# Hybrid decoder layer on one core: sample output product in three column parts, prompt probabilities scaled by GpSimd before plain transposes, value products two turns behind

## Chip, cores and metric

The kernel runs on one core of one Trainium2 chip. The metric is the device time of one execution in microseconds (us). The measurement tells a change of about 0.5% from none. Engines are named PE (TensorE; PEld is its weight load), DVE (VectorE), ACT (ScalarE), POOL (GpSimd) and SP (SyncE, which issues all DMAs here).

## What is computed

One decoder layer over a prompt (2048 positions) and 64 sample rows (8 sequences of 8 new positions, each with a cache of 2048). Model width 1024; the mixer has 6 attention heads of width 64 (A), an RG-LRU (B) and 6 HGRN2 heads (C). The change touches part A only, and of it two things: the prompt's attention after the softmax, and the product of probabilities and cached values for the samples.

```
h = rmsnorm(x); z = h @ w_in                     # q, k, v, gates of A, B and C
A, prompt: three strided branches per head, (window, dilation) = (128,1), (512,4), (2048,16)
    p_b = exp(q k^T / 8 - max_b);  o_b = p_b v / sum(p_b)
    o   = sum_b weight_b * o_b,  weight_b ~ denominator of branch b    (softmax over log-sum-exps)
    mixed_A = o * silu(gate)
A, sample: the same for 8 new rows of each of 8 sequences against cache + new keys
y = x + concat(mixed_A, mixed_B, mixed_C) @ w_out;  y = rmsnorm(y)
```

## The kernel before

The program has two parts. `front` (0 to about 1110 us of the profile) makes the input projections and parts B and C of the prompt; the change does not touch it. `attend_project` does the rest. Its order of work is a hand-written list of steps, made by `attend_schedule` and `project_schedule`; every engine walks the same list and issues its own share of each step, in order, and the engines meet at semaphores.

**Prompt attention.** The 2048 positions are held in 4 residue classes (position modulo 4), so that a row block `i` (0 to 3) is 512 positions. A head has 32 units `u` = (h, i, far, m): a unit is one 128-row score tile, near (128 or 256 keys) or far (128 times i+1 keys). For a unit PE makes two products (keys split into a high and a low part, L2446 and L2447) into one of three banks `sp_`, DVE adds the mask and takes the extreme (L2223), and ACT takes the exponential in place in the probability tiles `pna`, `pnb` and `pf` (L2071). After a head's last unit the steps `w`, `x` and `z` compute the merge weights of near and far, one number per query row and branch, in `wt` (L2160, L2284; semaphore `weights`).

Then come the head's 18 turns. A turn takes a group of up to four 128x128 probability blocks. Step `t` is one matmul for each block, with the block as stationary operand and a diagonal matrix as moving operand: this transposes the block and scales each query row by its weight at once (L2515, into bank `tp[n % 2]`). POOL makes the diagonals from the identity, eight per row block (L1978, tile `diag`). ACT copies three turns of four to `pt` in SBUF, DVE the fourth (L1601, L1603, in `evacuate`). Step `o` multiplies values and transposed block (L2538) into an accumulator `op` of 64 rows, those of the head's parity. In the list, `o` of turn n-1 follows `t` of turn n. When the four row blocks of a head are done, one after the other, each has a step `f`: DVE multiplies by the gate (L2294, 64x512) and SP stores it to the array `mab` (L1852). The turns of head h begin 11 units into head h+1 (`LEAD`), so they are laced with that head's units; those of the last head have no units beside them, only the nine steps `pw` that split `w_out` (ACT L2082, DVE L2300). The q and k of the next head are read and split in the steps `s` (ACT L2029, DVE L2208 and L2212).

**Projection and samples.** `project_schedule` laces 34 half-tiles `pp` of the output product (27 matmuls of 128x512 each, helper lines L49 to L51) with the attention of eight samples. For sample b: `sr` POOL multiplies 2304 columns of far keys by the query (L1992), `sk` scores, `sm` transposes the probabilities into `ptt`, `so` the output product (L2581): for each of 11 key tiles one matmul of all 48 probability columns (6 heads x 8 rows) with all 384 value columns, of which only a head's own 64 are used. DVE copies 48x384 to `orow` (L2360), `sb` turns it back in three transposes (L2587). `pt` and `split_mixed` prepare a tile of the mixed activations: its A part is read from `mab` once the stores of step `f` have landed (`load_mixed`).

## Time and profile before

| | |
|---|---|
| median of 3 runs | 1864.3 us (1863.65 to 1872.5) |
| profiled execution | 1865.9 us, of which span 1864.2 us |
| mean granted PE clock | 0.98 of 2.4 GHz |
| PE, DVE, ACT, POOL busy | 93%, 54%, 48%, 35% |
| prompt attention with turns | about 1222 to 1510 us |
| projection and samples | about 1510 to 1864 us |

Busy shares are averages over stages with different limits, so they say little about one stage. A record "MATMUL ... 0.27 us" is the latency of one pipelined matmul; what a matmul costs a stream is the distance from its start to the next one's start. A float32 product of two full operands shows as two records, a transpose through the identity as one.

### The profile page before, as it was taken

Reading aid. Unit: us, or ns where it says so; the run is one execution under the profiler, and the core shown is the slowest. Engines: PE = TensorE matmul, PEld = TensorE weight load, DVE = VectorE, ACT = ScalarE, POOL = GpSimd, SP = SyncE. Lnnn points to the kernel's source line nnn. Section 1 sums busy time; section 2 is a strip of 40 time slices with the busy share of each in tenths; the row PEclk is TensorE's granted clock in tenths of the full one; section 3 lists DMA queues with packets and bytes.
Section 4 is the critical chain, followed back from the end, with each engine's and each line's share of the span. In section 5 each row is a group of like instructions: output and inputs, shape, how many; then the busy total and the mean of one; then the engine's idle time right before and its main releaser. Section 6 shows DMA issues by size and latency. Waiting matters only on the chain. (4 is left out here: it accounts for less than half of the span.)

```text
span 1864.2 us, 38820 instructions
## 1 busy us (share of the span) xinstructions
PE 1727.1 (93%) x15435; PEld 1440.4 (77%) x15435; DVE 997.7 (54%) x2040; ACT 891.7 (48%) x1650; POOL 648.2 (35%) x876
## 2 busy tenths in 40 slices
PE   6989998999899999999899977999999998999998
PEld 5978887898777778787778867777788886666665
DVE  3436744312666676666766544455555466444542
ACT  4527773112566655677777734456555411111110
POOL 1102211100666566655666532044443511121110
PEclk9999998999999999999999998989999999999999
DMA  6310101223121121212111114364410365656541
GB/s 206 99 49 30 46 28 53 73 78 121 25 59 28 39 56 26 61 29 60 27 42 48 32 58 129 107 174 127 119 50 12 103 195 176 202 166 198 181 142 37
DMA packets 181793, 162.71 MB, mean 87 GB/s; under 512 B 65427, under 2 KB 168878, under 8 KB 180846
## 3 DMA queue, kind: packets, MB, share of 16 engines
q1 hardware_dynamic: 181614, 160.24, 28.9%
q8 instruction: 123, 2.02, 0.5%
q14 instruction: 56, 0.46, 0.1%
HBM read 116.89 MB, written 46.55 MB: 88 GB/s over the span
## 5 line engine op out<-in xcount | busy, mean ns | idle before, releaser
L49 PE MATMUL f_bank<-c_ht,c_whi 128*128 128x384 f32 (+1 forms) x864 | 321.4, 372 | 5.7 <-DVE c_wlo L863 5.7
L51 PE MATMUL f_bank<-c_ht,c_wlo 128*128 128x384 f32 (+1 forms) x864 | 303.4, 351 | 0.0
L50 PE MATMUL f_bank<-c_ht,c_whi 128*128 128x384 f32 (+1 forms) x864 | 303.2, 351 | 0.0
L812 ACT ACTIVATE f_scr<-f_scr 128x384 f32<-128x384 f32 (+1 forms) x210 | 114.4, 545 | 198.6 <-POOL f_scr L594 198.2
L1013 DVE TENSOR_TENSOR f_scr<-f_scr 128x192 f32<-128x192 f32 (+1 forms) x210 | 102.8, 490 | 182.0 <-ACT f_scr L812 181.8
L49 PEld LDWEIGHTS f_bank<-c_ht,c_whi 128*128 128x128 f32 x864 | 163.1, 189 | 21.4 <-DVE c_wlo L863 6.5
L1978 POOL TENSOR_SCALAR a_diag<-c_ident,a_wt 128x128 f32<-128x128 f32 x192 | 120.8, 653 | 155.6 <-DVE a_wt L2284 107.2
L50 PEld LDWEIGHTS f_bank<-c_ht,c_whi 128*128 128x128 f32 x864 | 163.6, 189 | 9.7 <-issue 1.1
L51 PEld LDWEIGHTS f_bank<-c_ht,c_wlo 128*128 128x128 f32 x864 | 163.3, 189 | 9.3
L593 POOL TENSOR_TENSOR f_scr<-f_scr 128x192 f32<-128x192 f32 (+1 forms) x210 | 135.9, 647 | 31.8 <-PE f_tps L1188 29.4
L1004 DVE COPY_PREDICATED f_scr<-f_scr,f_tps 128x384 f32<-128x384 int32 (+1 forms) x210 | 129.9, 619 | 13.1 <-PE f_tps L1188 4.0
L49 PE MATMUL a_s<-a_whi,a_mhi 128*128 128x512 f32 (+1 forms) x306 | 123.2, 403 | 4.7 <-DVE a_y L2377 4.7
L1188 PEld LDWEIGHTS f_tps<-f_scr 128*32 128x32 f32 (+1 forms) x5184 | 75.4, 112 | 58.1 <-issue 28.8
L50 PE MATMUL a_s<-a_wlo,a_mhi 128*128 128x512 f32 (+1 forms) x306 | 120.1, 393 | 0.0
L619 POOL TENSOR_SCALAR f_scr<-f_scr,c_lbl 128x384 f32<-128x384 f32 (+1 forms) x30 | 45.0, 1499 | 211.3 <-ACT f_scr L779 211.3
L1188 PE MATMUL f_tps<-f_scr 128*32 128x32 f32 (+1 forms) x5184 | 96.7, 200 | 19.1 <-DVE f_scr L1013 10.2
L1997 POOL TENSOR_TENSOR a_small<-a_small,c_mhalf 128x1 f32<-128x1 f32 (+1 forms) x17 | 9.4, 552 | 280.4 <-DVE a_small L2381 280.4
L49 PE MATMUL f_bank<-c_whi,c_ht 128*128 128x384 f32 x256 | 91.4, 357 | 4.0 <-DVE c_wlo L867 4.0
L51 PE MATMUL f_bank<-c_whi,c_ht 128*128 128x384 f32 x256 | 87.7, 343 | 0.0
L50 PE MATMUL f_bank<-c_wlo,c_ht 128*128 128x384 f32 x256 | 87.7, 342 | 0.0
L2071 ACT ACTIVATE a_pf<-a_pf,a_sf 128x128 f32<-128x128 f32 (+3 forms) x96 | 53.4, 557 | 66.3 <-DVE a_sf L2223 66.0
L49 PE MATMUL f_bank<-c_htail,c_whi 128*128 128x448 f32 x216 | 84.2, 390 | 0.0
(397 smaller groups left out, 4079.5 us busy)
## 6 DMA issues: line engine op xcount, KB each, us to landing
f_wraw<-in_w_in SPq DMA_DIRECT2D x27, 512.0 KB, 4.1
a_raw<-zf SPq DMA_DIRECT2D x48, 256.0 KB, 4.0
a_k<-in_ck SPq DMA_DIRECT2D x48, 192.0 KB, 3.3
a_v<-in_cv SPq DMA_DIRECT2D x48, 192.0 KB
f_scr<-in_xp SPq DMA_DIRECT2D x16, 512.0 KB, 4.5
a_x<-in_xp SPq DMA_DIRECT2D x16, 512.0 KB, 4.6
out_y_prompt<-a_y SPq DMA_DIRECT2D x16, 512.0 KB, 2.9
zt<-f_stage SPq DMA_DIRECT2D x38, 192.0 KB, 1.9
```

Of the source, the lines that this page charges most:

```text
L49: nc.tensor.matmul(out, w_hi, m_hi, start=start, stop=False)
L50: nc.tensor.matmul(out, w_hi, m_lo, start=False, stop=False)
L51: return nc.tensor.matmul(out, w_lo, m_hi, start=False, stop=stop)
L593: G.tensor_tensor(d[:, :, hs:], b[:, :, hs:], r, ALU.subtract)
L619: G.tensor_scalar(key[:, :n], key[:, :n], lbl[:, 1, h:h + 1], None, ALU.mult).then_inc(S["gated"], 1)
L812: A(lev[i % 3][:, :n], lev[i % 3][:, :n], ACT.Exp).then_inc(S["expd"], 1)
L1004: V.copy_predicated(attn[:, :n].rearrange("p (j t) -> p j t", t=P), m.bitcast(I32).unsqueeze(1).to_broadcast([P, nt, P]), lp[x % 2][:, :n] ...
L1013: V.tensor_tensor(e[:, :, hs:], e[:, :, hs:], q[:, :, hs:], ALU.mult).then_inc(S["xlev"], 1)
L1188: mm = nc.tensor.matmul(lp[x % 2][k0:k0 + w, queries], left[:, keys], right[:, queries], start=True, stop=True)
L1978: G.tensor_scalar(diag[:, 2 * NC * (b % 2) + NC * far + m, :], con["ident"][:], wt[h % 2][:, far, c:c + 1], None, ALU.mult).then_inc(S["di ...
L1997: G.tensor_tensor(s[:, 2:3], s[:, 1:2], con["mhalf"][:rows_of(n), 0:1], ALU.pow).then_inc(Z["rstd"], 1)
L2071: A(probs(n), probs(n), ACT.Exp, bias=stat(n, 0), scale=-1.0, accum_out=stat(n, 1)).then_inc(S["exped"], 1)
```

## The change

Four edits go together.

1. **Scaling moves.** The diagonals are gone. When a head's weights are there, POOL scales its probability tiles in place, ten `tensor_tensor` instructions per head in the order `SCALES` (near rows 0 and 1, far 0 and 1, near 3 and 2, far 3 and 2). Step `t` becomes a plain transpose through the identity.
2. **Lanes.** The four row blocks no longer follow one another: blocks of row blocks 0 then 3 (lane 0) alternate with those of 1 then 2 (lane 1). Lane 0 accumulates in rows 0 to 63 of `op`, lane 1 in rows 64 to 127, so successive value products go to different 64-column tiles of PE. A head now has two steps `f` of 128x512 in place of four of 64x512, and each stores with two DMAs; the gates are loaded in four DMAs for a head pair to match.
3. **Two turns behind.** `o` of turn n-2 follows `t` of turn n, and `f` moves back accordingly; `pm` and `pt 0` move a little later in the list.
4. **Sample output.** For each key tile three matmuls of 16 probability columns (two heads) with 128 value columns, into rows 0, 32 and 64 of the bank; three DVE copies of 16x128 and one transpose of 96 rows follow.

```
+LANES = ((0, 3), (1, 2))
+LANE, STEP = (0, 1, 1, 0), (0, 0, 1, 1)
+SCALES = [(0, 0, 0), (0, 0, 1), (0, 0, 2), (0, 1, 0), (1, 0, 0), (1, 1, 0), (0, 3, 0), (0, 2, 0), (1, 3, 0), (1, 2, 0)]
...
-        for i in range(SB):
-            blocks = [(0, a, j) for a in range(NC) for j in (NC * i + a, NC * i + a - 1) if j >= 0]
-            blocks += [(1, g, j) for g in range(NC) for j in range(i + 1)]
-            groups += [(h, i, blocks[b:b + 4]) for b in range(0, len(blocks), 4)]
+        rows = [[(i, far, a, j) for i in both for far in range(2) for a in range(NC) for j in block_keys(i, far, a)] for both in LANES]
+        blocks = [b for pair in itertools.zip_longest(*rows) for b in pair if b]
+        groups += [(h, blocks[b:b + 4]) for b in range(0, len(blocks), 4)]
...
-        if made:
-            order.append(("o", made - 1))
-        if made - 2 in ends:
-            order.append(("f", ends.index(made - 2)))
+        if made >= 2:
+            order.append(("o", made - 2))
+        if made - 3 in ends:
+            order.append(("f", ends.index(made - 3)))
...
-        if n == 8:
+        if n == 11:
             order.append(("pm", 0))
-        if n == 14:
+        if n == 16:
             order.append(("pt", 0))
...
-                    for far in range(2):
-                        for m in range(NC):
-                            c = m * SB + i
-                            G.tensor_scalar(diag[:, 2 * NC * (b % 2) + NC * far + m, :], con["ident"][:], wt[h % 2][:, far, c:c + 1],
-                                            None, ALU.mult).then_inc(S["diag"], 1)
+                    for far, i, part in SCALES:
...
+                        by_row = wt[h % 2][:, far, :].rearrange("p (m i) -> p m i", i=SB)[:, m0:m0 + ms, i]
+                        G.tensor_tensor(p, p, by_row.unsqueeze(2).to_broadcast([P, ms, w]), ALU.mult).then_inc(S["scaled"], 1)
...
-                        mm = nc.tensor.matmul(tp[n % 2][:, c * P:(c + 1) * P], prob_block(h, i, blk),
-                                              diag[:, 2 * NC * (b % 2) + NC * blk[0] + blk[1], :], start=True, stop=True)
+                        mm = nc.tensor.transpose(tp[n % 2][:, c * P:(c + 1) * P], prob_block(h, blk), ident[:])
...
+                        acc = op[STEP[i]][LANE[i] * HD:(LANE[i] + 1) * HD, :]
...
                 if i < NTILE:
-                    stored(sp, SB * (NH - 1) + i // NC)
+                    stored(sp, 2 * (NH - 1) + STEP[i // NC])
...
-                        mm = nc.tensor.matmul(ob[:R, 0:AW], ptt[:w, j, :], vv[:w, j, :], start=(j == 0), stop=(j == KT))
+                        for pr in range(3):
+                            mm = nc.tensor.matmul(ob[own_rows(pr), 0:P], ptt[:w, j, pr * 2 * NT:(pr + 1) * 2 * NT],
+                                                  vv[:w, j, pr * P:(pr + 1) * P], start=(j == 0), stop=(j == KT))
```

On PE, in the turns of head 2 among the units of head 3, this stands before (`a_s` are score products, `a_t` the transposing step, `a_o` the value products; a row's numbers after a name are buffers):

```order
L2515 MATMUL a_t<-a_diag,a_pf_16243 128x128 x4
L2538 MATMUL a_o<-a_pt_16256,a_vf_16254 64x128 x4
L2446 MATMUL a_s<-a_khi_16232,a_qst 128x256
L2447 MATMUL a_s<-a_klo_16234,a_qst 128x256
L2515 MATMUL a_t<-a_diag,a_pna_16248 128x128 x3
```

And this after:

```order
L2553 MATMUL a_t<-c_ident,a_pf_16243 128x128
L2553 MATMUL a_t<-c_ident,a_pf_16245 128x128
L2553 MATMUL a_t<-c_ident,a_pf_16243 128x128
L2553 MATMUL a_t<-c_ident,a_pf_16245 128x128
L2576 MATMUL a_o<-a_pt_16257,a_vf_16254 64x128 x4
L2485 MATMUL a_s<-a_khi_16232,a_qn 128x256
L2486 MATMUL a_s<-a_klo_16234,a_qn 128x256
```

A turn still has four instructions of each kind, but the blocks of two row blocks (tiles 16243 and 16245) alternate, and the value products read an older `a_pt`.

On DVE, in the last head, this stands before (`a_pt` are the copies of `evacuate`, `a_oa` the steps `f`, `a_wlo` the split of `w_out`):

```order
L1603 COPY a_pt_16259<-a_t 128x512
L2300 TENSOR_TENSOR a_wlo_16314<-a_wraw_16323,a_whi 128x1024
L2300 TENSOR_TENSOR a_wlo_16315<-a_wraw_16324,a_whi 128x1024
L2300 TENSOR_TENSOR a_wlo_16316<-a_wraw_16321,a_whi 128x1024
L2294 TENSOR_TENSOR a_oa_16264<-a_o,a_gs_16261 64x4x128
L2300 TENSOR_TENSOR a_wlo_16317<-a_wraw_16322,a_whi 128x1024
L1603 COPY a_pt_16259<-a_t 128x512
```

And this after:

```order
L1627 COPY a_pt_16259<-a_t 128x512
L2334 TENSOR_TENSOR a_wlo_16313<-a_wraw_16322,a_whi 128x1024
L2334 TENSOR_TENSOR a_wlo_16314<-a_wraw_16323,a_whi 128x1024
L2334 TENSOR_TENSOR a_wlo_16315<-a_wraw_16320,a_whi 128x1024
L2334 TENSOR_TENSOR a_wlo_16316<-a_wraw_16321,a_whi 128x1024
L1627 COPY a_pt_16259<-a_t 128x512
L2334 TENSOR_TENSOR a_wlo_16317<-a_wraw_16322,a_whi 128x1024
L2328 TENSOR_TENSOR a_oa_16262<-a_o,a_gs_16260 128x4x128
```

The last head has two steps `f` now instead of four. The copy of turn 99 (the second `a_pt` row) stands behind the sixth piece of `w_out`, and the store that the first mixed tile needs follows the `a_oa` of the last row, after the seventh.

On POOL, this stands where head 0's turns begin, before:

```order
L1958 TENSOR_TENSOR a_h_vb_16310<-a_h_vv,a_h_rowm 64x512
L1978 TENSOR_SCALAR a_diag<-c_ident,a_wt_16277 128x128 x32
L1978 TENSOR_SCALAR a_diag<-c_ident,a_wt_16278 128x128 x32
```

And this after, once per head:

```order
L2012 TENSOR_TENSOR a_pna_16242<-a_pna_16242,a_wt_16276 128x128
L2012 TENSOR_TENSOR a_pna_16242<-a_pna_16242,a_wt_16276 128x256
L2012 TENSOR_TENSOR a_pnb_16244<-a_pnb_16244,a_wt_16276 128x512
L2012 TENSOR_TENSOR a_pnb_16244<-a_pnb_16244,a_wt_16276 128x1024
L2012 TENSOR_TENSOR a_pf_16240<-a_pf_16240,a_wt_16276 128x512
L2012 TENSOR_TENSOR a_pf_16241<-a_pf_16241,a_wt_16276 128x1024
L2012 TENSOR_TENSOR a_pnb_16244<-a_pnb_16244,a_wt_16276 128x1024 x2
L2012 TENSOR_TENSOR a_pf_16243<-a_pf_16243,a_wt_16276 128x2048
L2012 TENSOR_TENSOR a_pf_16245<-a_pf_16245,a_wt_16276 128x1536
```

Thirty-two instructions on 128 columns become ten on 9088 columns in all, each with two inputs in SBUF.

## Rows read from the trace of the kernel before

**Rows 1.** The page, part 1: busy time, share of the span and instructions.

```profile
span 1864.2 us, 38820 instructions
PE 1727.1 (93%) x15435; PEld 1440.4 (77%) x15435; DVE 997.7 (54%) x2040; ACT 891.7 (48%) x1650; POOL 648.2 (35%) x876
```

**Rows 2.** Windows: length, busy us of PE, PEld, DVE, ACT, POOL, PE clock, DMA.

```profile
1265.50:1467.50 202.00, 188.88 (x1454) 164.47 (x1454) 106.39 (x343) 116.96 (x324) 77.52 (x128) 1.00 0.27 72
1467.40:1510.20 42.80, 42.80 (x328) 36.89 (x327) 21.16 (x23) 17.86 (x25) 22.79 (x32) 1.00 0.59 188
1510.20:1864.20 354.00, 339.37 (x1561) 225.68 (x1561) 168.21 (x264) 49.58 (x107) 56.94 (x30) 0.99 0.51 161
```

**Rows 3.** Line L2284 (the weights of a head): first and last start.

```profile
L2284 DVE COPY a_wt<-a_x x6: 175/175/176, 1214.2 to 1467.3; 128x16 f32<-128x16 f32 x6
```

**Rows 4.** Timeline of PE, two turns of the last head: start, length, group.

```profile
1490.00 1.16 PE L2515 MATMUL a_t<-a_diag,a_pf 128*128 128x128 f32 x8
1491.09 1.09 PE L2538 MATMUL a_o<-a_pt,a_vn 128*64 128x128 f32 x8
1492.10 1.16 PE L2515 MATMUL a_t<-a_diag,a_pf 128*128 128x128 f32 x8
```

**Rows 5.** Timeline of PE: transposes of a sample's keys, and what follows.

```profile
1586.60 0.66 PE L2402 MATMUL a_t<-c_ident,a_k 128*128 128x128 f32 x4
1587.19 0.71 PE L2419 MATMUL a_o<-a_selm,a_far_rows 128*48 128x16 f32 x12
```

**Rows 6.** Timeline of PE in `front`: products of 64 and of 32 columns.

```profile
719.74 0.29 PE L1204 MATMUL f_op<-f_scr 128*64 128x64 f32 x4
719.86 0.29 PE L1207 MATMUL f_op<-f_wbd,f_scr 128*64 128x64 f32 x4
...
707.16 0.55 PE L1285 MATMUL f_tps<-f_scr 128*32 128x64 f32 x24
707.53 0.37 PE L1188 MATMUL f_tps<-f_scr 128*32 128x32 f32 x24
```

**Rows 7.** Timeline of PE: one sample's output product, and what follows.

```profile
1604.73 7.42 PE L2581 MATMUL a_x<-a_v,a_ptt 128*48 128x384 f32 x22
1612.09 0.55 PE L2597 MATMUL a_s<-c_ident,a_m 128*128 128x128 f32 x3
```

**Rows 8.** POOL instructions by line: ns min/median/max.

```profile
L1992 POOL TENSOR_TENSOR a_k<-a_k,a_qrep x8: 5118/5468/6923, 1533.7 to 1775.0; 128x2304 f32<-128x2304 f32 x8
L1978 POOL TENSOR_SCALAR a_diag<-c_ident,a_wt x192: 594/607/1665, 1216.3 to 1491.4; 128x128 f32<-128x128 f32 x192
```

**Rows 9.** Timelines of POOL and DVE at 1567 us; line L2387 as a whole.

```profile
1567.18 5.12 POOL L1992 TENSOR_TENSOR a_k<-a_k,a_qrep 128x2304 f32<-128x2304 f32 x1
1567.24 6.13 DVE L2387 SCALAR_TENSOR_TENSOR a_y<-a_y,a_small,a_gfin 128x1024 f32<-128x1024 f32 x1 [0.66 <-POOL a_small L1997]
L2387 DVE SCALAR_TENSOR_TENSOR a_y<-a_y,a_small,a_gfin x17: 1269/1285/6134, 1533.8 to 1858.3; 128x1024 f32<-128x1024 f32 x16, 64x1024 f32<-64x1024 f32 x1
```

**Rows 10.** DVE instructions with two SBUF inputs, by line.

```profile
L2208 DVE TENSOR_TENSOR a_klo<-a_raw,a_khi x12: 1162/1225/1367, 1125.6 to 1387.3; 128x1024 fp32r<-128x1024 f32 x12
L2212 DVE TENSOR_TENSOR a_qst<-a_raw,a_qst x12: 1221/1223/1680, 1139.2 to 1420.1; 64x1024 fp32r<-64x1024 f32 x12
L2300 DVE TENSOR_TENSOR a_wlo<-a_wraw,a_whi x9: 1215/1225/1353, 1480.3 to 1497.0; 128x1024 fp32r<-128x1024 f32 x9
```

**Rows 11.** DMA issues: count, size, median us to landing.

```profile
a_mb<-mab SPq DMA_DIRECT2D x16, 384.0 KB, 5.0
mab<-a_oa SPq DMA_DIRECT2D x24, 128.0 KB, 2.9
```

**Rows 12.** Windows of 5 us, columns as in rows 2.

```profile
1070.00:1075.00 5.00, 2.08 (x9) 1.46 (x9) 3.81 (x7) 4.96 (x7) 1.37 (x2) 1.00 0.27 80
1075.00:1080.00 5.00, 4.32 (x15) 3.34 (x15) 4.96 (x8) 1.74 (x4) 3.48 (x5) 0.66 0.15 40
1215.00:1220.00 5.00, 4.11 (x9) 2.01 (x9) 4.90 (x11) 1.92 (x7) 5.00 (x6) 0.50 0.42 113
```

More of the change, by code:

```diff
@@ L1378, with block_keys, first_block, last_group @@
 KM = 3 * AW // P
+LANES = ((0, 3), (1, 2))
+LANE, STEP = (0, 1, 1, 0), (0, 0, 1, 1)
+SCALES = [(0, 0, 0), (0, 0, 1), (0, 0, 2), (0, 1, 0), (1, 0, 0), (1, 1, 0), (0, 3, 0), (0, 2, 0), (1, 3, 0), (1, 2, 0)]
+def block_keys(i, far, m):
+    if far:
+        return list(range(i + 1))
+    return [j for j in (NC * i + m, NC * i + m - 1) if j >= 0]
+def first_block(i):
+    return i, 0, 0, NC * i
+def last_group(groups, h, i):
+    return max(t for t, (g, blocks) in enumerate(groups) if g == h and any(b[0] == i for b in blocks))
 def attend_schedule():
@@ L1463, in attend_schedule @@
         turn()
-    order += [("o", made - 1), ("f", len(ends) - 1)]
+    order += [("o", made - 2), ("o", made - 1), ("f", len(ends) - 1)]
     return units, groups, ends, order + project_schedule()
@@ L1577, in stat, with prob_block @@
             return sn[h % 2][:, k, NC * i + m:NC * i + m + 1]
-        def prob_block(h, i, block):
-            far, m, j = block
+        def prob_block(h, block):
+            i, far, m, j = block
             if far:
@@ L1585, in prob_block, with scaled_by @@
             return near_block(h, own)[:, c:c + P]
+        def scaled_by(h, i, far, m):
+            part = min(m, 2) if (far, i) == (0, 0) else 0
+            return len(SCALES) * h + SCALES.index((far, i, part)) + 1
         owner = ["v" if t % 4 == 3 else "a" for t in range(len(groups))]
@@ L1772, in load_g @@
             def load_g(c):
-                sp.dma_start(gs[c % 2][:], zf[(ZGA + c) * P:(ZGA + c + 1) * P, 0:SEQ]).then_inc(g_in[c % 2], 16)
+                for hp in range(2):
+                    row = (ZGA + c) * P + hp * HD
+                    blocks = zf[row:row + HD, 0:SEQ].rearrange("p (s t) -> p s t", t=CLS)
+                    for lane, (i0, i1) in enumerate(LANES):
+                        dst = gs[c % 2][lane * HD:(lane + 1) * HD, hp * 2 * CLS:(hp + 1) * 2 * CLS].rearrange("p (s t) -> p s t", t=CLS)
+                        sp.dma_start(dst, blocks[:, i0:i1 + 1:i1 - i0, :]).then_inc(g_in[c % 2], 16)
             def far_of(cache, b, j):
@@ L1848, in _ @@
                 elif kind == "f":
-                    h, i, _ = groups[ends[n]]
-                    rows = slice((h % 2) * HD, (h % 2 + 1) * HD)
+                    h, step = n // 2, n % 2
                     sp.wait_ge(S["final"], BASE + n + 1)
-                    sp.dma_start(mab[h * HD:(h + 1) * HD, i * CLS:(i + 1) * CLS], oa[n % 2][rows, :]).then_inc(store[n % 2], 16)
-                    if (h, i) == (0, SB - 1):
+                    for lane, both in enumerate(LANES):
+                        i = both[step]
+                        sp.dma_start(mab[h * HD:(h + 1) * HD, i * CLS:(i + 1) * CLS],
+                                     oa[n % 2][lane * HD:(lane + 1) * HD, :]).then_inc(store[n % 2], 16)
+                    if (h, step) == (0, 1):
                         for name, tokens in (("v_win_prompt", slice(0, SEQ)), ("v_win_sample", slice(SEQ, T))):
                             sp.dma_start(io[name], zt[tokens, TV:TV + AW]).then_inc(H["windows"], 16)
-                    if (h, i) == (1, SB - 1):
+                    if (h, step) == (1, 1):
                         load_g(2)
@@ L1935, in _ @@
             assert hc.n == hgrn_const
-            started = -1
             for kind, n in order:
@@ new lines, in _ @@
+                    hp, c2 = h % 2, h // 2
+                    heads_cols = slice(hp * HD, (hp + 1) * HD)
+                    if n == 0:
+                        pe.wait_ge(VS["out"], BASE + NV)
+                    if blocks[0] == first_block(0):
+                        pe.wait_ge(v_in[c2 % 2], BASE + 16 * 2 * NC * (c2 // 2 + 1))
+                    begun = [2 * h + STEP[blk[0]] for blk in blocks if blk == first_block(blk[0])]
+                    if begun and max(begun) >= 2:
+                        pe.wait_ge(S["final"], BASE + max(begun) - 1)
@@ L2529, in _ @@
                     copied(pe, n)
-                    rows = slice(hp * HD, (hp + 1) * HD)
-                    for c, (far, m, j) in enumerate(blocks):
+                    for c, blk in enumerate(blocks):
+                        i, far, m, j = blk
+                        acc = op[STEP[i]][LANE[i] * HD:(LANE[i] + 1) * HD, :]
                         if far:
-                            out = op[b % 2][rows, m * P:(m + 1) * P]
-                            val = vf[c2 % 2][:, m * SB + j, rows]
-                        else:
-                            out = cls(op[b % 2][rows, :])[:, :, m * QR:(m + 1) * QR]
-                            val = vn[c2 % 2][:, j, rows]
-                        mm = nc.tensor.matmul(out, val, pt[n % 4][:, c * P:(c + 1) * P], start=first and c == 0,
-                                              stop=n in ends and c == len(blocks) - 1)
+                            out = acc[:, m * P:(m + 1) * P]
+                            val = vf[c2 % 2][:, m * SB + j, heads_cols]
+                        else:
+                            out = cls(acc)[:, :, m * QR:(m + 1) * QR]
+                            val = vn[c2 % 2][:, j, heads_cols]
+                        mm = nc.tensor.matmul(out, val, pt[n % 4][:, c * P:(c + 1) * P], start=blk == first_block(i),
+                                              stop=blk == (i, 1, NC - 1, i))
```

89 lines of the change are left out of this document (43 added, 46 removed).

## The prediction, made before the changed kernel ran

> **What bounds the kernel now.** I read the page first [rows 1]: PE is busy 93% of the span, so the question is where PE sets the pace and what comes next when it gets faster. The windows show it by stage [rows 2]. From 1265.5 to 1467.5 us, four heads with units and turns laced, PE is busy 188.9 of 202.0 us, ACT 117.0, DVE 106.4, POOL 77.5: 50.5 us a head, of which PE works 47.2, ACT 29.2, DVE 26.6. In the last head (42.8 us) and in the projection (354 us, PE 339.4) it is PE again. The weights of head 0 come at 1214.2 and those of head 5 at 1467.3 [rows 3].
>
> The timeline gives the cost of a turn by distances between starts [rows 4]: 1.09 us from step `t` to step `o`, 1.01 us from there to the next `t`, so 2.10 us. Eighteen turns are 37.8 us of a head's 50.5; units and the rest take the other 12.7.
>
> **Transposes.** A plain transpose is one record where the product with a diagonal is two. Four of them take 0.59 us before the next step begins (1586.60 to 1587.19) [rows 5], against 1.09 us: 0.50 us less a turn.
>
> **Value products on column tiles.** `front` already does this form of product. Four records of 64 moving columns, alternating between two 64-column tiles, take 0.12 us; 24 records on four 32-column tiles take 0.37 us [rows 6]. Eight records of 128 columns are four times the first: 0.48 us. To this comes a change of form between steps: today's eight records move 8 x 256 columns' worth of cycles, 0.85 us at the 2.4 GHz granted there, and need 1.01 us, so some 0.15 us. I take 0.61 for both, instead of 1.01. The new turn is 0.59 + 0.61 = 1.20 us, 0.90 less; a head's PE work falls from 50.5 to 12.7 + 18 x 1.20 = 34.3 us.
>
> **The scaling on POOL.** Ten instructions on 9088 columns. L1992, also a product of two SBUF inputs, takes 5118 ns at best for 2304 columns, 2.22 ns each [rows 8]; with 0.1 us apiece that is 21.2 us a head. Upper end: the diagonals' 607 ns for 128 columns, 4.7 ns each, 43 us a head. I take 2.22, the row with the same operation and long tiles. In a loop of 35 to 40 us this fits, and the order of `SCALES` is the order of need: the first turn needs four instructions (4.7 us after the weights) and comes six units later in the list; the last, far row 2, is needed by the 13th turn.
>
> **What POOL's long instructions do to DVE.** While L1992 ran for 5.12 us, a DVE instruction with two SBUF inputs that started 0.06 us after it took 6.13 us instead of 1.28 [rows 9]: it waited for POOL to finish. The Trainium skill, page "SBUF — State Buffer", section "Who interferes with whom", states this as an exclusive lock between the two engines, held for a whole instruction and won by whichever starts first; the trace agrees (6.13 against 1.28 us). The attention loop has such DVE instructions: the key and query splits L2208 and L2212, 1.2 us each [rows 10]. Three of the next head's four stand 8, 12 and 18 units behind the weights, where POOL is inside instructions of 2.4 to 4.7 us. At half of the running instruction each they wait about 1.2 + 2 + 1.8 = 5 us a head. Queued behind them on DVE are the score reductions, and for these wait PE (three banks) and ACT. The two longer steps `f` in place of four give DVE back some 2 us, off the path.
>
> So a head becomes 34.3 + 5.0 + 0.7 for waits on copies = 40 us. Its lower end is 35, if lanes and the spare turn absorb the blocking; its upper end 46, if every blocked split costs a whole POOL instruction and the pipeline refills slowly (three times about 4 us on 34.3). From the first dense turns at about 1225 us to the weights of head 5 there are 242 us or 4.8 heads: 4.8 x 10.5 = **50 us saved** (22 to 74).
>
> **The last head.** With PE alone it would fall from 42.8 to 18 x 1.20 = 22 us. It won't, for two reasons. POOL hands over far row 3 at 17.7 and far row 2 at 21.2 us after the weights, and nine splits of `w_out` (L2300, 1.22 us each [rows 10]) now fight it for the lock. I walk it: split 0 at 10.6, split 1 at 14.3, split 2 at 20.2, split 3 once far row 2 is done at 24.9, splits 4 and 5 to 28.6; only then comes the copy of turn 99, for which PE stands still, and seven turns of 1.2 follow: 38 us. Secondly, the first mixed tile needs the store of the step `f` that closes rows 0 and 1. This step now stands behind split 6, about 32 us in; store 2.9 us and load 5.0 us [rows 11] give 40, where the transposes `pt 0` block PE in the list with two `t` and four `o` behind them, 3.4 us: 43 to 44 us. What was 42.8 stays 43: **0 us saved** (-3 to +10).
>
> **Projection.** A sample's output product takes from 1604.73 to 1612.09 = 7.36 us [rows 7]. The new one has 33 products of 128 columns, 66 records on three tiles. From the 24 records of 64 columns on four tiles in 0.37 us [rows 6]: 15.4 ns x 2 for the columns x 4/3 for the tiles = 41 ns each, 2.7 us. Saved 4.7 x 8 samples = **37 us** (31 if records overlap only in pairs, 3.5 us each time; 39 if there is no loss). PE works 339 of 354 us there and DVE 168, so most of it should show. The Trainium skill, page "TensorE: Matmul & The Clock Gate", section "Part 3: Packing small matmuls — row/col tiling", gives 2.38x for three column tiles; by that the product would take 7.36 / 2.38 = 3.1 us and the saving would be 34, an estimate from that page. Three small copies replace one in front of a transpose that isn't waited for at once: nothing.
>
> **Sum.** 50 + 0 + 37 = 87 us off the profiled execution's 1865.9 us is 1779 us; the median of the three runs is 1.6 us lower, and I take 2 us back for moments at a low clock after the stand in the last head. **Predicted: 1780 us**, 4.5% faster. An experiment can tell about 0.5% (9 us) from no change.
>
> **Rivals.**
> - *Blocking costs little* (20%). The splits slip between POOL's instructions, the head runs at PE's 35 us: 74 + 5 + 38 gives about 1750 us. For it: ACT's 29.2 and DVE's 26.6 us leave room. Against it: DVE executes in order and has only three score banks before it.
> - *POOL becomes the bound* (12%). At the diagonals' 4.7 ns a column, or with reductions that read the mask also blocked, a head takes 46 to 49 us and the last head gets 5 us longer. Only the projection is left: 1815 to 1835 us. For it: L1978's rate and its maximum of 1665 ns [rows 8]; against it: L1992's rate on the same operation.
> - *Column tiles don't overlap at this size* (7%). Then `o` stays at 1.01 and the 33 products take 33 x 0.27 = 8.8 us: the loop gains 5 us a head at most (24), the samples lose 11: about 1850 us. Against it are rows 6.
> - *The clock falls* (5%), the one that ends slower. PE was granted full speed through the loop and the last head [rows 2], but after 5 us with 2.1 us of work it got 0.66, and at 1215 us 0.50, though PE counted as busy 4.1 of 5 us [rows 12]. If the loop, with PE idle at every blocked split, ran at 1.2 GHz, its 34.3 us would be 60 to 69; at 60, 4.8 x 9.5 = 46 us are lost, the last head 3, the projection 37 gained: 1878 us. It decides only if nine tenths of the loop are slow, since 87 us of gain stand against 4.8 x 20 us. The Trainium skill, page "TensorE: Matmul & The Clock Gate", section "Part 4: PE-mode transpose", says that transposes through the identity do not count as activity for the clock. Were it so here, this is the way it would come out; the rows with many transposes don't settle it.
>
> **How the numbers follow.** Forecast (contention of some 5 us a head, 1755 to 1812) 52%; the four rivals 20, 12, 7 and 5%; 4% for anything else. Leaving out the slow tail and a little below 1740, the range is **1738 to 1822**. Nearly all cases are faster by more than 0.5%: 0.93; same 0.03; slower 0.04.
>
> **What the changed profile would show.** A turn of 1.2 us where the last head runs freely; weights 40 us apart instead of 50.6, with PE's share there near 85% and waits of PE and ACT for DVE's reductions; POOL's ten instructions at 21 to 24 us a head; L2208 and L2212 with maxima of 3 to 6 us instead of 1.4 and 1.7; a stand of PE before the copy of turn 99 and before `pt 0`; the sample product at 2.7 us, eight times. Wrong it would be with a clock under 0.9 in the loop, a POOL rate over 3 ns a column, or sample products over 3.6 us.

## Result and the profile after

The changed kernel takes 1790.1 us (median of 4 runs, 1789.5 to 1796.1) where the kernel before, run beside it, takes 1866.3 (1863.7 to 1872.5): ratio 0.959, 95% interval 0.956 to 0.963. That is 76 us or 4.1% faster; 1780 was forecast, with a range of 1738 to 1822.

The page of the changed kernel, part 1, against [rows 1]; PE is busy for 91% of a shorter span, and was for 93%:

```profile
span 1788.1 us, 38488 instructions
PE 1623.2 (91%) x15345; PEld 1355.5 (76%) x15345; DVE 1000.4 (56%) x2044; ACT 888.0 (50%) x1650; POOL 628.4 (35%) x745
```

Windows of three steady heads, of the next, of the last head and of the projection (columns as in rows 2), first before, then after:

```profile
1267.20:1421.30 154.10, 142.26 (x1094) 123.76 (x1094) 83.01 (x266) 92.31 (x253) 58.87 (x96) 1.00 0.34 90
```

```profile
1270.40:1399.50 129.10, 106.78 (x879) 78.88 (x879) 79.36 (x261) 90.31 (x253) 54.05 (x30) 0.93 0.44 108
1399.50:1430.00 30.50, 28.75 (x267) 21.94 (x268) 19.18 (x74) 23.97 (x70) 16.71 (x10) 1.00 0.08 19
1430.00:1472.00 42.00, 32.65 (x255) 23.38 (x254) 22.28 (x23) 17.52 (x25) 17.67 (x10) 0.76 0.61 190
1472.00:1788.10 316.10, 299.90 (x1896) 222.10 (x1894) 170.54 (x280) 49.55 (x107) 53.11 (x31) 0.98 0.57 181
```

PE worked 92% of the steady heads before and works 83% of them now, at a mean clock of 0.93 of full instead of 1.00. So PE no longer sets the pace alone there. The heads are read from the copies that finish their weights, against [rows 3]; VectorE's timeline:

```profile
1217.45 0.17 DVE L2318 COPY a_wt<-a_x 128x16 f32<-128x16 f32 x1
1270.39 0.17 DVE L2318 COPY a_wt<-a_x 128x16 f32<-128x16 f32 x1
1313.92 0.17 DVE L2318 COPY a_wt<-a_x 128x16 f32<-128x16 f32 x1
1355.95 0.17 DVE L2318 COPY a_wt<-a_x 128x16 f32<-128x16 f32 x1
1399.50 0.18 DVE L2318 COPY a_wt<-a_x 128x16 f32<-128x16 f32 x1
1429.97 0.17 DVE L2318 COPY a_wt<-a_x 128x16 f32<-128x16 f32 x1
```

Between the first and the last lie 212.5 us; before, 1214.17 to 1467.35, 253.2. The balance of the two spans, 1864.2 and 1788.1: the first weights come 3.3 us later, the loop gives 40.7, the last head (from its weights to its last step `f`, 42.9 and 41.6) 1.3, the projection (354.0 and 316.5) 37.5. Together 76. The later start lies before anything that the change touches: the first split of keys after `front` (L2242) already starts 3.0 us later, at 1128.6 us instead of 1125.6.

One turn where nothing is waited for, and one sample's product, against [rows 4, 7]; PE's timeline:

```profile
1441.62 0.66 PE L2553 MATMUL a_t<-c_ident,a_pf 128*128 128x128 f32 x4
1442.21 0.66 PE L2576 MATMUL a_o<-a_pt,a_vn 128*64 128x128 f32 x8
...
1532.65 2.70 PE L2620 MATMUL a_x<-a_v,a_ptt 128*16 128x128 f32 x66
1535.28 0.50 PE L49 MATMUL a_s<-a_whi,a_mhi 128*128 128x512 f32 x1
```

The step after 1442.21 starts at 1442.80: a turn is 1.18 us by distances where the clock is full, and was 2.10. The sample product takes 2.63 us to the next record, and took 7.36.

### The profile page after: what moved, and what is told of

Read it like the earlier page. It is cut to its first block and busy times, and to the rows that moved or that the text cites. A ratio compares the mean times of both kernels' runs of the same rounds, so it can differ in the third digit from the quotient of the medians.

```text
span 1788.1 us, 38488 instructions
## 1 busy us (share of the span) xinstructions
PE 1623.2 (91%) x15345; PEld 1355.5 (76%) x15345; DVE 1000.4 (56%) x2044; ACT 888.0 (50%) x1650; POOL 628.4 (35%) x745
## 5 line engine op out<-in xcount | busy, mean ns | idle before, releaser
L593 POOL TENSOR_TENSOR f_scr<-f_scr 128x192 f32<-128x192 f32 (+1 forms) x210 | 135.6, 646 | 34.3 <-PE f_tps L1188 32.0
L1004 DVE COPY_PREDICATED f_scr<-f_scr,f_tps 128x384 f32<-128x384 int32 (+1 forms) x210 | 130.0, 619 | 14.4 <-PE f_tps L1188 5.4
L51 PE MATMUL f_bank<-c_whi,c_ht 128*128 128x384 f32 x256 | 88.6, 346 | 0.0
L49 PE MATMUL f_bank<-c_htail,c_whi 128*128 128x448 f32 x216 | 84.3, 390 | 0.0
L51 PE MATMUL a_s<-a_whi,a_mlo_a 128*128 128x512 f32 (+1 forms) x204 | 80.5, 395 | 0.0
L50 PE MATMUL f_bank<-c_htail,c_whi 128*128 128x448 f32 x216 | 79.3, 367 | 0.0
```

Source lines behind the costliest of these rows:

```text
L49: nc.tensor.matmul(out, w_hi, m_hi, start=start, stop=False)
L50: nc.tensor.matmul(out, w_hi, m_lo, start=False, stop=False)
L51: return nc.tensor.matmul(out, w_lo, m_hi, start=False, stop=stop)
L593: G.tensor_tensor(d[:, :, hs:], b[:, :, hs:], r, ALU.subtract)
L1004: V.copy_predicated(attn[:, :n].rearrange("p (j t) -> p j t", t=P), m.bitcast(I32).unsqueeze(1).to_broadcast([P, nt, P]), lp[x % 2][:, :n] ...
```

## The experiments

All numbers of heads in one place: the distances from the weights of one head to those of the next, the last head as above, and how the median stands to that of the kernel before in the same session (1865.9 to 1867.9 us; for the changed kernel 1866.3).

| kernel | us | ratio, 95% | 0-1 | 1-2 | 2-3 | 3-4 | 4-5 | last |
|---|---|---|---|---|---|---|---|---|
| before | 1866.3 | | 53.0 | 51.2 | 51.6 | 51.3 | 46.0 | 42.9 |
| changed | 1790.1 | .959 (.956-.963) | 52.9 | 43.5 | 42.0 | 43.5 | 30.5 | 41.6 |
| e1 sample product only | 1829.4 | .979 (.977-.981) | 52.9 | 51.2 | 51.6 | 51.3 | 46.0 | 42.9 |
| e2 attention only | 1823.8 | .977 (.975-.979) | 52.9 | 43.5 | 42.1 | 43.5 | 30.5 | 41.7 |
| e3 scale 8 columns | 1763.7 | .945 (.943-.947) | 44.9 | 39.5 | 41.0 | 41.0 | 31.2 | 33.6 |
| e4 rows in turn | 1797.5 | .962 (.961-.964) | 59.6 | 42.5 | 45.3 | 42.5 | 36.2 | 37.6 |
| e5 one turn behind | 1816.7 | .973 (.972-.975) | 60.5 | 48.2 | 50.6 | 48.1 | 34.1 | 41.1 |
| e6 short scaling | 1775.7 | .952 (.950-.953) | 47.7 | 42.6 | 40.1 | 44.4 | 32.7 | 34.1 |
| e7 half of copies on DVE | 1795.2 | .961 (.958-.964) | 57.3 | 44.7 | 44.7 | 43.8 | 33.0 | 38.3 |
| e8 narrow splits | 1763.1 | .945 (.944-.947) | 50.6 | 35.5 | 36.0 | 35.5 | 30.5 | 40.3 |
| e9 split steps apart | 1776.5 | .952 (.950-.954) | 47.8 | 40.9 | 40.5 | 40.8 | 35.3 | 41.3 |
| e10 = e6 + e9 | 1760.5 | .943 (.942-.945) | 40.9 | 40.0 | 39.6 | 40.8 | 35.2 | 34.3 |
| e11 = e10, rows in turn | 1768.5 | .948 (.947-.950) | 45.2 | 40.6 | 40.6 | 40.6 | 38.7 | 34.9 |
| e12 before, steps apart | 1852.0 | .992 (.991-.994) | 51.2 | 47.6 | 47.2 | 47.6 | 47.5 | 42.9 |

**Do the two parts add?** e1 applies the sample product's hunks to the kernel before; e2 takes them out of the changed one.

```diff
 (e1, on the kernel before)
-mm = nc.tensor.matmul(ob[:R, 0:AW], ptt[:w, j, :], vv[:w, j, :], ...)
+for pr in range(3):
+    mm = nc.tensor.matmul(ob[own_rows(pr), 0:P], ptt[:w, j, pr * 2 * NT:(pr + 1) * 2 * NT], vv[:w, j, pr * P:(pr + 1) * P], ...)
```

> The kernel before, with the edit of the sample output product alone: three matmuls of 128x16 by 128x128 on column tiles for each block of keys, three row copies, one transpose. Theory (the two parts of the change add): the projection stage loses 38 us (354.0 before, 316.1 after) and nothing else moves, so about 1828 us, 1824 to 1832. Rival (part of the stage's gain comes from a better start, since the attention loop before it leaves a higher clock or earlier loads behind): the stage gives 25 to 32 here, 1834 to 1841 us. The product itself: 2.7 us for 66 records as in the changed kernel.

> The changed kernel with the sample output product put back to one of 48 columns by 384: the attention edits alone. Theory (the parts add): 1790 plus 38, about 1828 us, 1823 to 1832; mean distance of two heads' weights 42.5 us, as in the changed kernel. Rival: if the product on column tiles costs or gives something outside its own stage, the sum of both runs' gains misses 76 us by more than 5.

e1 is 38.4 us faster than before, e2 44.1; their sum of 82.5 misses 76.2 by 6.3, just over the 5 that e2's rival was given. But the stages are the same to 0.5 us (the loop 212.5 in e2 as in the changed kernel, the projection 316.0 in e1 and 316.5 there): in e2 the first weights came at 1212.2 us instead of 1217.4, and that is most of the difference.

Where does this start come from? The first split of keys starts between 1122.6 and 1128.6 us in the fourteen profiles (1128.6 in the changed kernel, 1123.4 in e2), though no edit touches what stands before it. That part is scatter of `front`, and what causes it stays open. From this split to the first weights it is 88.6 to 88.9 us in eight kernels, 90.9 in e6 and e7, and 85.3 to 87.6 in e9 to e12. So the parts add, and a difference of a few us between two of these kernels is read from the stages, not from the total.

**What does GpSimd's work cost?**

```diff
 (e3)
+p = p[:, :, 0:8]
 _, ms, w = p.shape
 (e6)
+SCALES = [(0, 0, 0, 1), (0, 0, 1, 2), (0, 0, 2, 4), (0, 1, 0, 2), (0, 1, 2, 4), (1, 0, 0, 4), (1, 1, 0, 2), (1, 1, 2, 4)]
+SCALES += [(0, i, m, m + 2) for i in (3, 2) for m in (0, 2)] + [(1, i, m, m + 1) for i in (3, 2) for m in range(4)]
```

> The changed kernel, but GpSimd scales only the first 8 columns of each group of probabilities: most of the scaling is left out (the other columns stay unscaled), every wait stays. It takes GpSimd's 17.7 us a head and VectorE's waits behind it away together. Theory P (GpSimd's work is what makes a head 42.5 us instead of 34 to 36, by VectorE's blocked splits and by the wait for scaled blocks): heads at 36 us or less, 1790 minus 30 or more, 1745 to 1762 us. Theory C (the head is set by the turns, scores, reductions and exponentials that wait for each other in order, whatever GpSimd does; the one split of 8.4 us is all that its lock costs): heads at 41 to 42.5, 1776 to 1788 us. I hold C to be likelier, since the splits in the loop but one took 1.3 to 2.4 us against 1.2 unblocked.

> The changed kernel with GpSimd's scaling cut into 20 instructions of at most 512 columns a head instead of 10 of up to 2048; same work, same order. Theory L (VectorE stands until the GpSimd instruction under way ends, so its wait goes with the instruction's length): the split of 8.4 us falls to under 3, the two of the last head from 6.3 to about 3, and most of the 8 us that the first head and the 8 us that the last head gave back with the scaling left out come back here too, less about 0.1 us for each further instruction: 1790 minus 6 to 14, 1776 to 1784 us. Rival M (VectorE gets no turn between GpSimd instructions that follow each other, whatever their length): nothing is gained, 1788 to 1793 us, and the split still takes over 6 us.

e3 gives 26 us, between the two theories; 4.4 of it lie before the first split. By the table, three steady heads lose 7.5 us together, 2.5 each: they stay at 39.5 to 41.0, near C's 41 and far from P's 36. But head 0-1 loses 8.0 and the last head 8.0, which C did not have. What happens in head 0-1 of the changed kernel, in the timelines of GpSimd and of VectorE, and in PE's waits from 1217 to 1271 us (total, times, longest):

```profile
1228.96 3.75 POOL L2012 TENSOR_TENSOR a_pnb<-a_pnb,a_wt 128x1024 f32<-128x1024 f32 x2
1232.68 6.31 POOL L2012 TENSOR_TENSOR a_pf<-a_pf,a_wt 128x2048 f32<-128x2048 f32 x2
```

```profile
1231.64 8.42 DVE L2242 TENSOR_TENSOR a_klo<-a_raw,a_khi 128x1024 fp32r<-128x1024 f32 x1 [1.68 <-ACT a_khi L2063]
1239.99 0.41 DVE L2257 CUSTOM_DVE_ANT_0 a_pnb<-a_s,a_nmask 128x256 f32<-128x256 f32 x1
```

```profile
PE a_s L2485 <- DVE a_sn L2257: 8.0, 2, 7.4
```

The split began in the middle of one GpSimd instruction and ended 1.07 us after the third had ended: it sat through the rest of one and the whole of the next two. The reductions of the scores queued behind it, and PE stood 7.4 us for them. The Trainium skill, page "SBUF — State Buffer", section "Who interferes with whom", says that the engine that issues first holds the shared ports for its whole instruction. The trace agrees on the lock. But here it held for longer than one instruction: a waiting VectorE did not get in between two that follow each other (8.42 us; the longest single one of that head took 3.60).

That is the exception, not the rule. In the changed kernel six splits met a GpSimd instruction that another followed at once. Five of them got in at the first end, and then it was GpSimd's next instruction that took about 1 us longer, as here (4.60 us for the 2048 columns that took 3.60 in head 0-1):

```profile
1365.42 2.29 DVE L2242 TENSOR_TENSOR a_klo<-a_raw,a_khi 128x1024 fp32r<-128x1024 f32 x1 [1.76 <-ACT a_khi L2063]
```

```profile
1366.59 4.60 POOL L2012 TENSOR_TENSOR a_pf<-a_pf,a_wt 128x2048 f32<-128x2048 f32 x1
```

The split of head 0-1 sat through two ends again in e2 and in e9, 8.60 us both times. What decides whether VectorE gets in was not tested.

With twenty short instructions (e6) the longest split of keys takes 3.31 us instead of 8.42, and the longest split of `w_out` 2.06 instead of 3.77:

```profile
L2242 DVE TENSOR_TENSOR a_klo<-a_raw,a_khi x12: 1161/1726/3310, 1126.2 to 1363.7; 128x1024 fp32r<-128x1024 f32 x12
...
L2334 DVE TENSOR_TENSOR a_wlo<-a_wraw,a_whi x9: 1246/1795/2056, 1433.7 to 1449.3; 128x1024 fp32r<-128x1024 f32 x9
```

e6 is 14 us faster than the changed kernel: 5.2 in head 0-1, 7.5 in the last head and nothing in the four distances between (159.8 us together, and 159.5). L gave 6 to 14, M nothing; L holds, at its edge: the median is 14.4 us lower, and the longest split takes 3.31 us where under 3 was expected, since it sat through the ends of two short pieces. The edit has a side effect: a transposing step now waits for a smaller piece of GpSimd's work. It is not where the gain comes from: PE's waits for GpSimd go from 2.0 to 1.2 us in the last head and from 0.9 to 3.4 in head 0-1, where its waits for VectorE's reductions fall from 8.0 to 2.1. GpSimd itself pays: its last two groups in the last head take 14.04 us in eight pieces, against 7.30 in two.

**Do the column tiles and the second turn do what they are for?**

```diff
 (e4; SCALES in that order too)
-rows = [[(i, far, a, j) for i in both ...] for both in LANES]
-blocks = [b for pair in itertools.zip_longest(*rows) for b in pair if b]
+blocks = [(i, far, a, j) for i in (0, 1, 3, 2) for far in range(2) for a in range(NC) for j in block_keys(i, far, a)]
 (e5)
-if made >= 2:
-    order.append(("o", made - 2))
+if made:
+    order.append(("o", made - 1))
```

> The changed kernel with the blocks of a head in another order: row block 0, then 1, 3 and 2, each whole before the next (GpSimd scales in that order too), so that two value products that follow each other write the same column tile. All else stays: transposes, two turns behind, waits. Theory (the product's 0.59 us for 4 comes from overlap of the two column tiles): four products take about 1.0 us as before, a turn 1.6 us, 18 x 0.4 = 7.4 us of TensorE a head; where TensorE sets the pace (last head) 7 us, in the loop all of it too if TensorE is the bound: 1790 + 6 x 7.4 = 1834 us, range 1815 to 1840. Rival N (the products were 1.01 us before because each alternated with something else or was only one turn behind, and the lanes give nothing): a product stays at 0.6 us for four and the time within 5 us of 1790.

> The changed kernel with the value products one turn behind the transposes, as before, not two; column tiles and scaling stay. Between the transposes of a turn and its products then lie only the products of the turn before and the next transposes, 1.18 us, for a copy that ScalarE or VectorE makes in 0.58 or 0.69 us after whatever it has to do first. Theory T (the second turn hides copies that come late behind exponentials and splits): 1 to 2 us a head more in the loop, 1790 plus 5 to 15, 1795 to 1805 us. Rival U (the waits for copies only move to the transposes, which wait for the buffer of two turns before in either order): 1785 to 1793 us.

In e4 a step `o` stands where its four blocks share a column tile for 1.02 us (PE's timeline of its last head):

```profile
1442.34 1.09 PE L2575 MATMUL a_o<-a_pt,a_vf 128*64 128x128 f32 x8
1443.36 0.55 PE L2552 MATMUL a_t<-c_ident,a_pna 128*128 128x128 f32 x3
```

Against 0.59 with lanes: 0.43 us a turn, as both expectations of the mechanism had it. Yet only 7.4 us of time came of it, not 44, and the three steady heads take 130.3 us, against 129.0 with lanes. The theory is right on the overlap and wrong on its worth; N is wrong on the overlap and, with its 5 us, near on the worth. The overlap is nearly worthless where PE waits anyway, and part of it is taken back by PE's clock: in the same three heads that is 0.99 in e4 and 0.93 with lanes (e11 below has the sum). It shows in head 0-1 (59.6, not 52.9) and in head 4-5 (36.2, not 30.5), which has no splits. The last head is 4 us shorter without lanes: GpSimd's order differs there too, and the copy for which PE stands comes 16.2 us after the weights instead of 18.9.

e5 costs 27 us, twice the middle of what T gave it (5 to 15). PE now waits for the copies in front of the products, 15.5 us in 14 times for ScalarE and 8.0 in 4 times for VectorE between 1300 and 1420 us:

```profile
PE a_o L2576 <- ACT a_pt L1625: 15.5, 14, 2.6
...
PE a_o L2576 <- DVE a_pt L1627: 8.0, 4, 3.8
```

T holds, with a size that counted only the shortest delay of a copy.

**What does a steady head wait for, then?**

```diff
 (e7)
-owner = ["v" if t % 4 == 3 else "a" for t in range(len(groups))]
+owner = ["v" if t % 2 else "a" for t in range(len(groups))]
 (e8, in the steps s of ScalarE and VectorE)
+wide = half.stop - half.start if h < 2 else QR
+half = slice(half.start, half.start + wide)
```

> The changed kernel with every second group of transposes copied by VectorE, not every fourth. Theory A (ScalarE, 128.5 us busy of 179.3 in the loop, is what a head waits for): it gives 4.5 copies of 0.58 us a head to VectorE, up to 2.6 us a head, 1775 to 1783 us. Theory V (VectorE's latency, with its reductions behind which the next scores wait, is what a head waits for): 4.5 copies of 0.69 us more before its reductions, 1795 to 1808 us.

> The changed kernel, but the splits of keys and queries into a high and a low half work on 32 columns of each class instead of 256 from the third head on: most of that work of ScalarE (6 copies of about 1.06 us a head) and VectorE (4 of 1.22 us) is left out, the waits stay, old keys and queries are used. Theory S (in a steady head TensorE has 34 us of work and waits the rest for scores' reductions that stand behind these splits): steady heads fall from 42 to 43.5 to 36 to 38 us, 1790 minus 3 x 5 to 6 and some, 1768 to 1778 us. Rival R (the ring of three score banks paces the head by the latency of reduction and score in turn, splits or not): heads stay over 40.5 us, 1782 to 1790 us.

The time of e7 can't be told from that of the changed kernel (intervals .958 to .964 and .956 to .963). By stages its loop is 11 us longer, 4.4 in head 0-1 and 4.2 in the three steady heads, and its last head 3.3 shorter. So ScalarE's load is not the limit, and V, with 1795 to 1808, is the nearer. e8, which leaves out most of the work of the splits and computes with old keys, takes 27 us off, more than S said; 6 of them lie in `front`. Its steady heads are 35.5 to 36.0, at the lower end of S, and three of them have PE at full clock:

```profile
1261.80:1368.80 107.00, 98.18 (x885) 74.37 (x884) 69.26 (x261) 77.27 (x254) 50.45 (x30) 1.00 0.54 130
```

So 7.5 us of each steady head hang on the four splits; by the clock of 1.00 instead of 0.93, PE's slower work is a part of these 7.5. How, one place in the changed kernel shows; VectorE's timeline and then PE's:

```profile
1328.09 2.14 DVE L2242 TENSOR_TENSOR a_klo<-a_raw,a_khi 128x1024 fp32r<-128x1024 f32 x1 [1.74 <-ACT a_khi L2063]
1330.15 0.68 DVE L1627 COPY a_pt<-a_t 128x512 f32<-128x512 f32 x1
```

```profile
1330.97 0.41 PE L2553 MATMUL a_t<-c_ident,a_pf 128*128 128x128 f32 x2 [2.59 <-DVE a_pt L1627]
```

```profile
1330.00:1335.00 5.00, 4.03 (x25) 3.09 (x27) 3.12 (x12) 3.66 (x11) 2.84 (x1) 0.66 1.11 231
1335.00:1340.00 5.00, 4.40 (x41) 3.26 (x38) 2.31 (x6) 2.98 (x7) 0.00 (x0) 1.00 1.24 241
```

VectorE stands 1.74 us for ScalarE's copy of the same keys, then splits for 2.14 us, 0.9 of it for GpSimd, and only then copies the transposes for which PE stands 2.59 us. After that stand PE's transposes run 0.21 us apart instead of 0.11, at the 1.2 GHz level, until 1334.7. Only a part of such a delay is GpSimd's; the first part stands in the order of the steps, in which a step's two engines wait for each other. e9 takes that apart:

```diff
 (e9; VectorE runs "sd", ScalarE's copy into qn runs "se")
-if h and h + 1 < NH and k in (12, 16, 22):
-    order.append(("s", 4 * (h + 1) + (12, 16, 22).index(k)))
-if h and k == 4:
-    order.append(("s", 4 * h + 3))
+for kind, at, head in (("s", (12, 16, 20), h + 1), ("sd", (13, 17, 21), h + 1), ("se", (0, 0, 22), h + 1)):
+    if h and head < NH and k and k in at:
+        order.append((kind, 4 * head + at.index(k)))
+if h and k in (4, 5, 6):
+    order.append((("s", "sd", "se")[k - 4], 4 * h + 3))
```

> The changed kernel with the steps of a split of keys or queries taken apart from the second head's own on: ScalarE's copy stands where it stood (the third of a head at unit 20 instead of 22), VectorE's subtraction one unit of scores later, ScalarE's reordered copy of the queries one unit later again. Same work. Theory W (of the 7.5 us a head that narrow splits gave, most is the waiting of VectorE for ScalarE's copy, 22 us in 12 times over three heads, and of ScalarE for VectorE's subtraction, 7.7 us in 6 times, not their work): steady heads fall from 42 to 43.5 to 37 to 39 us, 1790 minus 10 to 20, 1770 to 1780 us. Rival D (it is the work, 4.9 us of VectorE and 6.3 of ScalarE a head, that delays reductions and copies wherever it stands): heads at 42 and more, 1786 to 1794 us.

> The short scaling instructions and the steps taken apart, both. If both theories hold and add: 1775.7 minus 10 to 18, 1758 to 1766 us. If the waits overlap (a late VectorE was hidden by the same TensorE idle time): 1768 to 1776 us.

> Short scaling instructions and steps taken apart, but the blocks in the order 0, 1, 3, 2 of row blocks, so that successive value products share a column tile. Theory E (column tiles gave only 7 us in the changed kernel because its steady heads wait for something else; where the wait is gone TensorE paces again and 18 x 0.42 = 7.5 us a head come out): e10 plus 15 to 35 us. Rival F (heads are still paced by the engines' waits): e10 plus 5 to 12.

> The kernel before with the steps of the splits taken apart in the same way. Theory G (heads of before are 51.3 to 51.6 us with 50.5 of TensorE work, so the waits of VectorE and ScalarE for each other were covered there and became the bound only with the change): nothing, 1863 to 1869 us. Rival H (they cost there too): 5 us a head less, 1845 us or less.

e9 is 14 us faster in time, but W's heads of 37 to 39 are 40.5 to 40.9: 122.2 us for three instead of 129.0, so some 2.3 of the 7.5 a head were this waiting. The other distances need care, because the edit moves the mark itself. The copy that ends a head's weights stood behind a split of queries, and now stands before it; VectorE's timeline, the changed kernel and then e9:

```profile
1216.19 1.22 DVE L2246 TENSOR_TENSOR a_qst<-a_raw,a_qst 64x1024 fp32r<-64x1024 f32 x1 [1.51 <-ACT a_qst L2063]
1217.45 0.17 DVE L2318 COPY a_wt<-a_x 128x16 f32<-128x16 f32 x1
```

```profile
1210.79 0.17 DVE L2322 COPY a_wt<-a_x 128x16 f32<-128x16 f32 x1
...
1212.70 1.37 DVE L2250 TENSOR_TENSOR a_qst<-a_raw,a_qst 64x1024 fp32r<-64x1024 f32 x1
```

This holds for heads 0 to 4 and not for head 5, which has no split beside it: part of the 4.8 us that head 4-5 is longer is this shift, in e10 to e12 too. From the first split of keys to the weights of head 5 e9 takes 293.0 us instead of 301.4, and 5.4 us of its gain lie in `front`: the edit is worth some 8 to 9 of the 14. W is half right; the work of the splits, or what it pushes aside, keeps the other 5. e10 gives 30 us, a little more than e6 and e9 together (28), by the same count 19.6 us to the weights of head 5 and 7.3 in the last head. It is the fastest kernel with the whole computation: 1760.5 us.

e12 was the surprise, and lies between its theories. The kernel before gains 14 us from the same edit (ratio .991 to .994), 15 by stages, and its steady heads fall from 51.4 to 47.5 us. G falls, and H's 5 us a head are 4: PE did stand around the splits before. With the steps apart it doesn't:

```profile
1262.40:1404.80 142.40, 141.63 (x1095) 123.66 (x1094) 83.06 (x269) 92.01 (x253) 65.75 (x96) 1.00 0.36 97
```

The same work of PE, 141.6 us and before 142.3, is done in 142.4 us instead of 154.1. e11 lands at e10 plus 8 us: F, not E. Its windows beside those of e10, three heads each (e10 first):

```profile
1253.20:1373.60 120.40, 106.66 (x883) 78.83 (x882) 78.09 (x263) 89.96 (x255) 62.28 (x60) 0.93 0.45 116
```

```profile
1255.10:1377.00 121.90, 117.44 (x882) 94.27 (x882) 78.77 (x263) 89.84 (x254) 63.27 (x60) 1.00 0.44 114
```

Without lanes PE is busy 96% of the time at full clock. With them it has 3 x 18 x 0.43 = 23 us less to do, is busy 10.8 us less, and finishes 1.5 us earlier. A clock of 0.93, with the two levels of 1.0 and 0.5, is 14% of the time at the lower one; half of that work, some 8 us in three heads, is what the low level adds. The same sum on e8, at 1.00, gives 98.2 us of work, which is e10's 106.7 less those 8. Another 9 us went into waits (PE idle 13.7 us in e10, 4.5 in e11), and some 4 of the 23 don't come out of this sum.

## Why the prediction was right, and where its steps were not

The turn, the sample product and the path of the last head came as forecast. The loop gave 10 us less, and that it was not more is in part an error that helped: head 4-5 gave 5 us more than its share.

**Turn, transposes, value products.** 1.20 us forecast, 1.18 measured. **GpSimd's rate.** 21.2 us a head forecast from [rows 8], 17.7 measured (10 instructions from 1430.21 to 1447.88 in the last head), 1.94 ns a column.

**The loop, 50 us saved: measured 40.7.** A head was to lose 10.5 us. Head 0-1 lost 0.1, the three steady heads 25.0 together (31.5 forecast), head 4-5 (no splits, the end of the units) 15.5. Two steps failed.

In head 0-1, of which the forecast counted 0.8 at the steady rate, PE was busy 42.7 us instead of 50.0 and the time stayed: it stood 8.0 us for reductions behind the split of 8.42 us, and its clock was 0.76, where it had been 0.89; the two were not separated. e10, without the long GpSimd instructions and with the steps apart, has 40.9 us there.

In the steady heads the step that failed is "units and the rest take the other 12.7", with the 34.3 us of PE's work built on it. It took all that was no turn for work of PE. Before, PE worked 47.4 of 51.4 us there, and e12 shows that the missing 4 were waits around the splits, which an edit of the order removes. Waits of this kind remain in the changed kernel (e9 takes 2.3 us a head of them out), so they belonged in the new sum as waits. The window that would have told was read, and passed over: PE busy 188.9 of 202.0 us [rows 2].

**The lock, 5 us a head.** The mechanism held; the size was uneven. e3 puts it at 2.5 us in steady heads and 8.0 in the first, 15 over the loop where about 24 were forecast. Half a running instruction per split was too much where GpSimd was nearly done, and too little where VectorE had to sit through three instructions. What is absent from the prediction's sum is the mean clock of 0.93, and that 7.5 us of a head hang on the splits as a whole. Had PE's waits been counted, 31 (47.4 less 18 times 0.92) + 4 + 2.5 us would still be 5 us short of the 43 measured; the clock explains at most some 3 of these, and the remainder is open.

**The last head, 0 us: measured 1.3.** The path was the one forecast, by the store and load behind the first step `f`, with other times on it. That step came 27.4 us after the weights instead of 32, at 1457.39; PE stood for the load until 35.3 us instead of 40. The stand before a copy came too, but before the copy of turn 95, 18.9 us in, which followed the split that had waited for GpSimd's last instruction. The copy of turn 99 came at 25.7 us, and nothing stood for it:

```profile
1449.71 0.45 PE L2553 MATMUL a_t<-c_ident,a_pnb 128*128 128x128 f32 x1 [4.50 <-DVE a_pt L1627]
1465.26 0.47 PE L2635 MATMUL a_s<-c_ident,a_m 128*128 128x128 f32 x1 [2.49 <-DMA a_mb<-mab]
```

From the load to the last step `f` it then took 6.3 us instead of 3.4, partly at the lower clock. That level stood for some 6.8 us at each of PE's three stands in this head (2.03 us for GpSimd at 1434.1, and these two). A turn takes 2.10 us there, as before the change (PE's timeline, where the next transposes start at 1440.39):

```profile
1438.29 1.12 PE L2553 MATMUL a_t<-c_ident,a_pnb 128*128 128x128 f32 x4
1439.34 1.12 PE L2576 MATMUL a_o<-a_pt,a_vn 128*64 128x128 f32 x8
```

```profile
1433.80:1440.50 6.70, 6.40 (x35) 4.42 (x36) 1.78 (x2) 1.19 (x2) 6.70 (x5) 0.50 0.71 275
1447.40:1454.20 6.80, 4.49 (x26) 3.19 (x27) 5.67 (x5) 2.80 (x4) 0.49 (x1) 0.50 0.60 202
1464.50:1471.20 6.70, 5.94 (x39) 4.96 (x40) 2.71 (x5) 1.09 (x2) 0.00 (x0) 0.50 0.96 259
```

Half of PE's 16.8 us of work in the three windows (columns as in rows 2), some 8 us, is what the lower level adds to its work. Most of it runs beside GpSimd's scaling and the splits: e9 spends 13.7 us of its last head at that level instead of 20.5, and the head is 41.3 us instead of 41.6. e6 shows that GpSimd's long instructions were the costly part. With short ones the copy of turn 95 comes 12.2 us after the weights, the first step `f` 22.1 us, and 7.5 us of this head came back.

**Projection, 37 us: measured 37.5.** e1 alone has 38.0. The product's 2.7 us was 2.63, 2.8 times less than before; the prediction's other estimate, 3.1 us and a saving of 34, was a little low.

**The rivals.** "Blocking costs little" would have needed PE's pace of 35 us; only e8, without most of the splits, comes near it. "POOL becomes the bound" fell with its rate. "Column tiles don't overlap" is refuted by 0.59 against 1.02 us. "The clock falls" was right in kind, at a fraction of its price: 0.93 in the steady heads, worth at most some 3 us each, 0.76 in head 0-1 and in the last head. From the first weights to those of head 5 the mean is 0.90, and was 0.98: just not "under 0.9 in the loop", which the prediction had as a sign of being wrong. The low stretches that were looked at, one in a steady head and three in the last, came with stands of PE of 2.0 to 4.5 us. e11, with the same number of transposes in three heads, ran at 1.00, so these alone don't bring the clock down.

**Open.** Why a steady head takes 40 us in e10, with PE's work at full clock near 33, ScalarE at 30 and VectorE at 26, was not settled; e3, without GpSimd, has the same 41. Which of work and position of the splits costs the last 5 us wasn't separated either. What decides whether a waiting VectorE gets in between two GpSimd instructions wasn't tested. And the low clock's cost was worked out, not isolated: no run changed it alone.

## What to carry to other kernels

Before a saving on the bounding engine is counted, its time must be split into work and waits, by a window over a few turns of the steady loop: the waits need not shrink with the work. Where two engines share a lock, the one that runs long instructions back to back should run short ones; that gave 14 us here. Where one step of a schedule has two engines in sequence, their halves belong at different places of the list, so that neither stands in order for the other; that gave 14 us to the kernel before, and to the changed one 14 by the time and some 9 by its stages.

## What was not expected of the hardware

- A VectorE instruction with two SBUF inputs sat through the rest of one GpSimd instruction and the whole of the next two, 8.42 us in all, and did not get in between; five others in the same kernel did, at the first end. With pieces of at most 512 columns the longest took 3.31 us.
- Four products of 128 columns that alternate between two 64-column tiles take 0.59 us, and 1.02 on one tile; the time of the kernel moved by 8 us for a PE saving of some 45 (18 turns, six heads, 0.43 us).
- Less work made a slower clock: 1.00 with PE 96% busy (e11), 0.93 with it 89% busy (e10), with the same steps but for the order of the blocks. What sets the level was not tested.
